# A hybrid decoder step on one core: the first rounds' small loads of the sample attention requested on ScalarE's queue

## The reference, cut to what matters

```python
def dilated_group_sample(q, k_all, v_all, window, dil, offset):
    t = q.shape[1]
    nk = window // dil + 1
    idx = offset + jnp.arange(t)[:, None] - dil * jnp.arange(nk)[None, :]
    ...
    sc = jnp.einsum('bthe,btjhe->bthj', q, kg, preferred_element_type=F32) * ATT_SCALE
    sc = jnp.where(valid[None, :, None, :], sc, -jnp.inf)
    lse = jax.nn.logsumexp(sc, axis=-1)
    pr = jnp.exp(sc - lse[..., None])
    o = jnp.einsum('bthj,btjhe->bthe', pr, vg.astype(F32))
    return o, lse
```

## Time and profile before

| | us |
|---|---|
| median of 3 runs | 4523.69 (4519.02 to 4526.64) |
| the profiled execution's own time | 4523.65 |
| its span, first to last instruction | 4521.9 |
| PE busy, of the span | 4243.1 (94%) |
| DVE busy | 1632.2 (36%) |
| ACT busy | 789.8 (17%) |
| sample attention, within the span | 3315.2 to 3446.0 (130.8) |

### The profile page before, as it was taken

How to read it: one execution, slowest core, us unless ns; L and a number is a source line. 1 busy time by engine, 2 the same in 40 slices (tenths; PEclk the granted TensorE clock), 3 DMA queues, 4 the chain that set the end, 5 groups by cost and what they waited for, 6 DMA issues and landing times. The chain is left out here.

```text
span 4521.9 us, 76759 instructions
## 1 busy us (share of the span) xinstructions
PE 4243.1 (94%) x34224; PEld 2866.0 (63%) x34224; DVE 1632.2 (36%) x2684; ACT 789.8 (17%) x1893; POOL 143.9 (3%) x145
## 2 busy tenths in 40 slices
PE   5999799999989999999997999999937999999998
PEld 2566588888866666666565666666625666666556
DVE  6000377666533433332012235454532433333001
ACT  1000222222102111111011222222212211111000
POOL 0000000000001000000000000000000100000001
PEclk8999899999889999999998999999968999999999
DMA  1122200011020111111222111111054011111223
GB/s 62 54 71 77 67 26 26 30 33 34 9 100 1 39 34 39 39 35 61 102 102 82 46 35 46 45 35 46 32 209 185 24 39 35 39 39 33 106 99 129
DMA packets 85444, 264.73 MB, mean 59 GB/s; under 512 B 37000, under 2 KB 43528, under 8 KB 76552
## 3 DMA queue, kind: packets, MB, share of 16 engines
q1 hardware_dynamic: 85128, 259.96, 16.6%
HBM read 224.34 MB, written 35.58 MB: 57 GB/s over the span
## 5 line engine op out<-in xcount | busy, mean ns | idle before, releaser
L279 PE MATMUL ps<-sb_h,sb_w 128*128 128x384 f32 (+1 forms) x4224 | 1289.8, 468 | 1.8 <-issue 1.8
L279 PEld LDWEIGHTS ps<-sb_h,sb_w 128*128 128x128 f32 x4224 | 801.7, 190 | 485.2 <-issue 2.8
L311 PE MATMUL ps<-sb_big,sb_w 128*128 128x384 f32 (+1 forms) x2112 | 646.6, 468 | 1.2 <-ACT sb_tmp L398 1.2
L1461 PE MATMUL ps<-sb_h,sb_w 128*128 128x384 f32 (+1 forms) x1728 | 575.8, 479 | 16.1 <-DMA sb_tmp<-c_amask 13.6
L311 PEld LDWEIGHTS ps<-sb_big,sb_w 128*128 128x128 f32 x2112 | 400.2, 190 | 241.6 <-ACT sb_tmp L398 2.2
L1461 PEld LDWEIGHTS ps<-sb_h,sb_w 128*128 128x128 f32 x1728 | 315.9, 192 | 197.9 <-issue 29.4
L486 DVE COPY sb_tmp<-sb_tmp 128x2 f32<-128x2 f32 x88 | 14.9, 169 | 760.9 <-ACT sb_tmp L398 760.9
L620 PE MATMUL ps<-sb_big,sb_w 128*128 128x384 f32 (+1 forms) x768 | 234.5, 468 | 0.0
L417 DVE TENSOR_TENSOR sb_tmp<-sb_tmp 128x384 f32<-128x384 f32 (+1 forms) x63 | 34.8, 552 | 526.4 <-ACT sb_tmp L343 524.7
L395 ACT ACTIVATE sb_tmp<-ps 128x384 f32<-128x384 f32 x176 | 86.2, 490 | 731.8 <-PE ps L279 731.8
L620 PEld LDWEIGHTS ps<-sb_big,sb_w 128*128 128x128 f32 x768 | 145.8, 190 | 88.5 <-issue 0.5
(11 more groups left out here) (244 smaller groups left out, 4151.6 us busy)
## 6 DMA issues: line engine op xcount, KB each, us to landing
sb_w<-wdown SPq DMA_DIRECT2D x46, 1408.0 KB, 6.0
sb_w<-wup SPq DMA_DIRECT2D x88, 512.0 KB, 3.6
sb_w<-wqkv SPq DMA_DIRECT2D x36, 512.0 KB, 3.6
sb_big<-kT SPq DMA_DIRECT2D x8, 2304.0 KB, 13.9
sb_big<-vc SPq DMA_DIRECT2D x8, 2304.0 KB, 15.6
rkv_scratch<-sb_w SPq DMA_DIRECT2D x24, 544.0 KB, 2.7
sb_w<-wrkv SPq DMA_DIRECT2D x24, 512.0 KB, 3.5
sb_x<-xT SPq DMA_DIRECT2D x2, 4352.0 KB, 18.2
```

The costliest lines, as they stand in the source:

```text
L279: mm = pe.matmul(m.ps[:, 3 * q + b, 0:n], wt[f % 2][q][:, k, :], m.H[:, k, t0:t0 + n], start=(k == 0), stop=(k == KT - 1))
L311: mm = pe.matmul(m.ps[:, u % 6, 0:n], wdt[u % 2][:, f, :], hid[:, f, t0:t0 + n], start=(f == 0), stop=(f == FT - 1))
L1461: mm = pe.matmul(m.ps[:, ring(s, p), 0:w], wt[t][:, k, :], m.H[:, k, t0:t0 + w], start=(k == 0), stop=(k == KT - 1))
```

## The change

On SyncE's queue the stage now starts with the four large requests alone: keys 0 and 1, values 0 and 1. The three loads of new rows, the four requests of the base mask and the eight of the mask columns of rounds 0 and 1 are requested on ScalarE's queue, ahead of its first wait. From the wait for the scores of round 0 on (`sfull`) SyncE's queue is as it was; the mask columns of rounds 2 and 3 stay on it. No wait is added or removed, and sizes and shapes are the same.

```diff
@@ sync
-            keys(0, 0)
-            for n, t in enumerate((q12, k12, v12)):
-                sp.dma_start(t.rearrange("p g c t -> p (g c) t"), scratch[n].rearrange("n p t -> p n t")).then_inc(qkv_in, 16)
-            keys(0, 1)
-            by_lane(0, 0, sum(CW), mask, base_in)
-            by_lane(0, P, 320, mnew[0], mk[0])
+            for b in range(2):
+                keys(0, b)
             for b in range(2):
                 vals(0, b)
-            by_lane(1, P, 320, mnew[1], mk[1])
             for i in range(1, ROUNDS):
                 sp.wait_ge(sfull, i)
@@ scalar
+            def by_lane(rnd, lo, hi, dst, signal):
+
+                src = a["c_smask"][rnd, :, lo:hi].rearrange("(b c r) k -> c b r k", b=2, c=AP_)
+                for c in range(AP_):
+                    act.dma_start(dst[lane(c)], src[c]).then_inc(signal, 16)
+
+            for n, t in enumerate((q12, k12, v12)):
+                act.dma_start(t.rearrange("p g c t -> p (g c) t"), scratch[n].rearrange("n p t -> p n t")).then_inc(qkv_in, 16)
+            by_lane(0, 0, sum(CW), mask, base_in)
+            by_lane(0, P, 320, mnew[0], mk[0])
+            by_lane(1, P, 320, mnew[1], mk[1])
             for g in range(3):
                 act.wait_ge(vtfull, g + 1)
```

## The result

The changed kernel takes 4534.85 us (median of 15 runs, 4525.22 to 4541.11) against 4523.64 for the kernel before (15 runs, 4518.88 to 4526.64): a ratio of 1.0027, 95% interval 1.0019 to 1.0034. It is slower by 11 to 12 us, where 11.7 were forecast. Its profiled execution is one of the shorter ones, 4531.74 us with a span of 4529.9.

What follows compares the result with a forecast made beforehand. Sample attention was taken to hang on when round 1's scores begin: 14.5 us later, less 2.8 given back, is +11.7 on 4523.65, so 4535.4 us. The 8 in 10 range was 4520 to 4543.

Steps and rivals of the forecast that it cites:

- What bounds the stage: Sample attention: its end hangs on when round 1's scores begin; rounds 1 to 3 then chain for 68.9 us.
- Turns of whole packets: Engines alternate packets of both queues, so new rows wait behind keys and values: in at 3345.6 against 3329.4.
- The overtaking: Round 1's keys pass round 0's last mask packets on the two mask engines; DVE released at 3372.9, 20.6 us later.
- Rival 1: Masks are not overtaken, so not slower: +0.5 us, 4524.2, range 4520 to 4529; chance 0.32.
- From the mask to round 1: From DVE's release by round 0's mask to the end of `place`: 18.7 us, kept as before.
- What is given back: Rounds 1 to 3 run shorter, 66.1 against 68.9, as PE idles less and a 1.5 us key wait goes: 2.8 us.
- Rival 3: ScalarE's copies come late or large packets lose overlap: adds 3 to 8 us, 4538 to 4544; within the forecast's 0.58.
- Rival 2: New rows and masks pass ahead of large loads: at best 10.1 us saved, 4513.5, likely 4519; chance 0.07.

Runs made afterwards that it cites:

- sp_values_first: Kernel before, still one queue, with round 0's values requested ahead of the masks; 4521.6 us, ratio 1.0.
- rows_act: Kernel before with only the new rows requested on ScalarE, SyncE asking for both keys, masks, then values; 4537.1 us, ratio 1.0031.
- after_third: The changed kernel, unedited, profiled a third time; 4534.4 us (one run).
- keys_held: Changed kernel with SyncE waiting for round 0's mask before requesting round 1's keys; 4526.5 us, ratio 1.0007 to the kernel before.

## Why the prediction was right, step by step

**What bounds the stage** held. From the start of round 1's scores to the end of the stage it is 68.7 to 70.0 us in every profile but two: 66.2 in sp_values_first, 73.2 in rows_act.

**Turns of whole packets** held to the packet (358 to 358). Rows in at 30.6, 30.8, 30.6, forecast 30.4; first scores 34.3, forecast 33.9. The evidence for it in the trace of before, one 16 KB packet of instructions that passed whole, was thin but pointed the right way. The rule of the Trainium skill ("DMA: Bandwidth & Descriptors", section "Queues, rings and completion order"), turns at the granularity of a packet, agrees with the trace in kind and not in size: the page counts some 9 to 17 descriptors to a turn, while here each turn was a single run of 256 bytes, 768 bytes, 5 KB or 18 KB. In after_third the small packets came 6 in each 2 us from 3357 to 3365, 3 an engine, and not in bursts.

**The overtaking** is right in mechanism and was treated as certain when it is a race. I had the keys of round 1 asked for at 40.3 us, when the mask's last packets were still out. At 40.8 they pass them and the mask comes at 58.1 to 58.2, forecast 57.7. At 41.6, in the first profile, they pass only a few, and it is 49.0. So the test that I had set for a wrong overtaking, L1884 before 3365 or 49.8 us after the start, was met there although the overtaking was at work. Rival 1, nothing overtaken, had the mask at 46.5; keys_held, where nothing can pass, has 45.4. Rival 1 drew from it a stage of 131; keys_held's was 133.5 and the first profile's 136.1, as nothing was given back.

**From the mask to round 1** took 17.4 to 17.7 us, not 18.7: the weighing (L1831, L1826 after) was over in 8.0 us, not 8.9. I did not follow that further.

**What is given back** was mis-sized: 2.8 us forecast, none measured (69.3 and 69.4 against 68.9). I had said that keys "have by then a start". Those of round 2 had none. Between round 1's scores and round 3's the engines stand at a share of 1.00 and 416 to 419 GB/s; a round's four requests (9.44 MB) are 22.6 us at that rate, and rounds 1 and 2 took 23.2 each. The DMA engines had no slack left there. The 1.5 us wait for keys went from before round 3 to before round 2 (PE ends `place` at 3404.4 and begins the scores at 3406.1). Before, rounds 1 and 2 with that wait were 46.7; now 46.4.

So in the full case round 1's scores begin 0.8 us earlier than forecast (75.6 against 76.4) and what follows is 3.2 us longer: stage 144.8 and 144.9 against 142.5, 14 us over the kernel before and not 11.7. The first profile's stage is 5.2 us over it. The median, +11.2, lies between the two cases. That it falls within 0.6 us of the forecast is in part luck: I had one case with too much given back, and the runs are a mixture, in a share that isn't known.

**Rival 3** did not come: ScalarE's three copies ended before the exponential was wanted in all three profiles (3360.9 against 3368.9 in the first), and the large packets still moved at 412 GB/s in turns with the rows. **Rival 2**, the small loads pass first, is what the change seems made for and is the opposite of what turns do.

## What to carry to other kernels

A second request queue doesn't give small loads a lane of their own: each packet of the one queue waits for a packet of the other on every engine that both use, so a load of many small packets beside a queue of large ones moves at one small packet for each large one. Count packets on each engine, not bytes. And when a small load holds up the chain, look first at how many of the sixteen engines carry it: here a wider shape gave 14 us where no order of the requests gave any.

## What the runs showed of the hardware

- Two data queues on one DMA engine alternate packet by packet, whatever the sizes: 358 to 358 (256 bytes and 18 KB), 47 to 47 and 59 to 59 (256 bytes and 5 KB).
- The mask requests over 32 partitions, laid out as two outer groups of 16, ran at a share of 0.13, two engines of sixteen; the same bytes over 128 partitions took 2.9 us, not 13.1.
- A request keeps its engine while its queue's backlog drains. ScalarE stood 27.3 us in three requests and 15.7 us in twelve. The other queue was not held by it: meanwhile SyncE's first four took 1.9 us together. A backlog on two engines is enough to hold a load for all sixteen: ScalarE's third request of rows in rows_act stood 12.6 us, at a share of 0.13.
- Between profiles of one kernel a difference of 0.8 us in one request, which came from the granted clock of the matmuls before it (0.71 or 0.84), decided 9 us, since large packets that arrive before the last small ones put themselves in front of each.
